# A two-layer hybrid model on one core: the first weight tile loaded ahead of x, x in two transfers with its norm weights, and the mixer's tiles multiplied high parts first

## The reference

```python
def rmsnorm(x, g):
    xf = x.astype(jnp.float32)
    y = xf * lax.rsqrt(jnp.mean(xf * xf, axis=-1, keepdims=True) + EPS)
    return (y * g.astype(jnp.float32)).astype(x.dtype)

def short_conv_mixer(h, w_in, conv_w, w_out):
    bg, cg, v = jnp.split(h @ w_in, 3, axis=-1)
    return (bg * causal_dwconv(cg * v, conv_w)) @ w_out

def conv_ffn(h, w_up, conv_w, w_down):
    u = causal_dwconv(h @ w_up, conv_w)
    a, g = jnp.split(u, 2, axis=-1)
    return (jax.nn.silu(a) * g) @ w_down

...
    for layer in range(DEPTH):
        if layer < N_A:
            x = x + short_conv_mixer(rmsnorm(x, mix_norm[layer]), a_w_in[i], a_conv[i], a_w_out[i])
        else:
            ...
            x = x + nsa_mixer(rmsnorm(x, mix_norm[layer]), b_w_qg[i], b_w_o[i], kv, rel_bias)
        x = x + conv_ffn(rmsnorm(x, ffn_norm[layer]), ffn_up[layer], ffn_conv[layer], ffn_down[layer])
    return rmsnorm(x, final_norm)
```

## Time and profile before

| what | value |
|---|---|
| median of three runs | 632.47 us (631.91 to 633.13) |
| the profiled execution's own time | 633.22 us |
| its span, first to last instruction | 631.5 us |
| PE busy | 610.9 us, 97% |
| DVE, ACT, POOL busy | 485.1, 388.6, 59.4 us |
| mean granted TensorE clock | 0.994 |
| DMA, mean over the span | 173 GB/s |

### The profile page before, as it was taken

The page is one execution under the profiler, slowest core; times in us unless marked ns, Lnnn a source line. Parts: engine busy times, 40 slices in busy tenths (PEclk is TensorE's granted clock), DMA queues, the critical chain, the costliest instruction groups (busy, mean ns, idle before and its releaser), DMA issues.

```text
span 631.5 us, 11277 instructions
## 1 busy us (share of the span) xinstructions
PE 610.9 (97%) x3738; PEld 534.1 (85%) x3738; DVE 485.1 (77%) x939; ACT 388.6 (62%) x708; POOL 59.4 (9%) x78
## 2 busy tenths in 40 slices
PE   7999999999999999999999898998999999999995
PEld 7999997888888888888989776777888888888884
DVE  4787756788888777777878789847788888777865
ACT  6644445666666666668556478717766666666644
POOL 0110002000000000011131144421000000000010
PEclk8999999999999999999999999999999999999998
DMA  8797432465656555761476400033365555555531
GB/s 310 290 336 241 179 133 100 166 203 194 205 201 202 199 189 179 287 241 34 146 245 214 142 2 2 1 101 133 118 206 193 209 201 207 192 178 195 199 101 66
DMA packets 30640, 109.55 MB, mean 173 GB/s; under 512 B 3419, under 2 KB 3691, under 8 KB 30476
## 3 DMA queue, kind: packets, MB, share of 16 engines
q1 hardware_dynamic: 30044, 106.97, 48.6%
q0 software_dynamic: 560, 2.12, 0.9%
HBM read 108.00 MB, written 1.07 MB: 173 GB/s over the span
## 4 chain that ended last, share of the span: by engine, by line
PE 88%; DVE 5%; ACT 3%; issue 2%; POOL 1%; DMA 1%; SPq 0%; DVEq 0%; ACTq 0%
PE bank L1129 24%; PE bank L1090 15%; PE bank L1091 15%; PE bank L1092 15%; PE bank L1133 13%; POOL work L486 1%; PE bank L1109 1%; DVE work L1013 1%; PE bank L1362 1%; DMA staged<-in_a_up 1%; ACT work L533 1%; PE bank L1320 1%; PE bank L1150 1%; PE bank L1110 1%; ACT w_hi L529 1%
## 5 line engine op out<-in xcount | busy, mean ns | idle before, releaser
L746 DVE TENSOR_TENSOR w_lo<-staged,w_hi 128x1024 fp32r<-128x1024 f32 x191 | 236.6, 1247 | 41.9 <-ACT w_hi L529 41.9
L529 ACT ACTIVATE w_hi<-staged 128x1024 fp32r<-128x1024 f32 x197 | 199.8, 1046 | 26.6 <-PE bank L1092 15.7
L1129 PE MATMUL bank<-gx,w_hi 128*128 128x512 f32 x672 | 167.2, 391 | 0.0
L1129 PEld LDWEIGHTS bank<-gx,w_hi 128*128 128x128 f32 x672 | 123.2, 188 | 23.8
L1133 PEld LDWEIGHTS bank<-gx,w_lo 128*128 128x128 f32 x672 | 91.7, 190 | 6.6
L1133 PE MATMUL bank<-gx,w_lo 128*128 128x256 f32 x672 | 93.7, 282 | 0.0
L1090 PE MATMUL bank<-w_hi,y 128*128 128x512 f32 x208 | 81.5, 392 | 0.0
L1091 PE MATMUL bank<-w_lo,y 128*128 128x512 f32 x208 | 81.5, 392 | 0.0
L1092 PE MATMUL bank<-w_hi,y 128*128 128x512 f32 x208 | 80.9, 389 | 0.0
L615 ACT ACTIVATE work<-work,params 128x256 f32<-128x256 f32 x96 | 44.2, 504 | 57.4 <-DVE work L847 39.2
L1090 PE MATMUL bank<-gx,w_hi 128*128 128x256 f32 x256 | 73.4, 287 | 2.6 <-DVE w_lo L746 2.1
(11 more groups left out here) (160 smaller groups left out, 818.7 us busy)
## 6 DMA issues: line engine op xcount, KB each, us to landing
staged<-in_f_up SPq DMA_DIRECT2D x88, 512.0 KB, 5.2
staged<-in_f_down SPq DMA_DIRECT2D x44, 512.0 KB, 3.3
staged<-in_a_up SPq DMA_DIRECT2D x24, 512.0 KB, 7.3
staged<-in_b_up SPq DMA_DIRECT2D x24, 512.0 KB, 4.3
staged<-in_a_down SPq DMA_DIRECT2D x8, 512.0 KB, 3.5
staged<-in_b_down SPq DMA_DIRECT2D x8, 512.0 KB, 4.2
bias<-bias_rows POOLq DMA_DIRECT2D x1, 2048.0 KB, 11.5
bias<-in_xT SPq DMA_DIRECT2D x4, 256.0 KB, 5.2
```

The costliest lines, as they stand in the source:

```text
L529: nc.scalar.activation(w_hi[:, q["slot"], 0:n], staged[:, s, 0:n], ACT.Copy).then_inc(hi, 1)
L746: nc.vector.tensor_tensor(w_lo[:, q["slot"], 0:n], staged[:, s, 0:n], w_hi[:, q["slot"], 0:n].bitcast(F32), ALU.subtract).then_inc(lo, 1)
L1129: nc.tensor.matmul(dst, w_hi[:, s, kt * P:kt * P + P], gx[:, kt, :], start=kt == 0, stop=False, skip_group_check=True)
```

## The change

It has four parts. The order in which SP issues the first loads is another: the first weight tile stands ahead of x, and the small parameters behind tile (1, 0). The transposed x comes in two transfers of four tiles each instead of four of two, and the first carries the eight columns of norm weights in front, which `norm_a` now reads instead of `params`; its lines are 4128 bytes long, those of the second 4096. `norm_a` handles tile (0, 0) ahead of the x tiles on ACT and DVE, and ACT puts tile (1, 0) between the two squares. `product` keeps its old order for piece (0, 0) alone; every other piece waits for `w_hi` only, issues its 16 matmuls with `w_hi`, then waits for `w_lo` and issues the other eight. PE makes piece (1, 0) ahead of `spread`, and `WARM` goes from 18 to 13.

```diff
-WARM = 18
+WARM = 13
...
-        x_first = bias[:, 0:KT, :]
+        x_lines = bias[:].rearrange("p h t -> p (h t)")[:, 0:KT + KT * T]
+        x_first = x_lines[:, KT:].rearrange("p (k t) -> p k t", k=KT)
...
             def x_tiles(b):
-                sp.dma_start(x_first[:, 2 * b:2 * b + 2, :], xT[:, 2 * b:2 * b + 2, :]).then_inc(x_landed[b], 16)
-
+                cols = slice(b * (KT + 4 * T), KT + (b + 1) * 4 * T)
+                sp.dma_start(x_lines[:, cols], xT[:, cols]).then_inc(x_landed[b], 16)
+
+            load("a", "up", 0, 0)
             x_tiles(0)
-            sp.dma_start(params[:], par).then_inc(par_landed, 16)
             x_tiles(1)
-            load("a", "up", 0, 0)
-            x_tiles(2)
-            x_tiles(3)
             load("a", "up", 0, 1)
             load("a", "up", 0, 2)
...
-            ups("a", 1)
+            load("a", "up", 1, 0)
+            sp.dma_start(params[:], par).then_inc(par_landed, 16)
+            load("a", "up", 1, 1)
+            load("a", "up", 1, 2)
...
             def norm_a():
 
-                act.wait_ge(par_landed, 16)
-                for b in range(4):
+                lead("a", "up", 0, 0)
+                for b in range(2):
                     act.wait_ge(x_landed[b], 16)
-                    for kt in (2 * b, 2 * b + 1):
+                    for kt in range(4 * b, 4 * b + 4):
                         nc.scalar.activation(gx_hi[:, kt, :], x_first[:, kt, :], ACT.Copy,
-                                             scale=gain(GAIN_OF["a"], kt)).then_inc(gx_hi_done, 1)
-                    if b == 1:
-                        lead("a", "up", 0, 0)
+                                             scale=x_lines[:, kt:kt + 1]).then_inc(gx_hi_done, 1)
...
                     if t:
+                        lead("a", "up", 1, 0)
                         act.wait_ge(squared, 1)
...
-                for c in range(3):
+                for c in (1, 2):
                     lead("a", "up", 1, c)
+                act.wait_ge(par_landed, 16)
...
             def norm_a():
 
-                dve.wait_ge(par_landed, 16)
+                rest("a", "up", 0, 0)
                 for kt in range(KT):
...
-                    if kt == 3:
-                        rest("a", "up", 0, 0)
                 rest("a", "up", 0, 1)
                 rest("a", "up", 0, 2)
+                rest("a", "up", 1, 0)
                 dve.wait_ge(deviated, 1)
...
             def product(q, dst, xh, xl, first, move=0, fresh=None, hi_sem=None):
 
                 s = q["slot"]
+                if fresh is not None:
+
+                    pe.wait_ge(lo_up, q["n"] + 1 + move)
+                    for kt in range(KT):
+                        pe.wait_ge(fresh, hi_sem + kt + 1)
+                        mm = three(dst, w_hi[:, s, kt * P:kt * P + P], w_lo[:, s, kt * P:kt * P + P],
+                                   xh[:, kt, :], xl[:, kt, :], first and kt == 0, kt == KT - 1)
+                    mm.then_inc(used_up, 1)
+                    return
+                pe.wait_ge(hi_up, q["n"] + 1 + move)
+                for kt in range(KT):
+                    for n, xs in enumerate((xh, xl)):
+                        nc.tensor.matmul(dst, w_hi[:, s, kt * P:kt * P + P], xs[:, kt, :], start=first and kt == 0 and n == 0, stop=False,
+                                         skip_group_check=True)
+
                 pe.wait_ge(lo_up, q["n"] + 1 + move)
                 for kt in range(KT):
...
+                    mm = nc.tensor.matmul(dst, w_lo[:, s, kt * P:kt * P + P], xh[:, kt, :], start=False, stop=kt == KT - 1,
+                                          skip_group_check=True)
                 mm.then_inc(used_up, 1)
...
                     up_a(0)
+                    up_a(1, cs=(0,))
                     spread()
...
-                    up_a(1)
+                    up_a(1, cs=(1, 2))
```

More of the change, by code:

```diff
@@ L221, in build @@
         landed = [sem(f"landed{s}") for s in range(UP_SLOTS + 1)]
-        x_landed = [sem(f"x_landed{b}") for b in range(4)]
+        x_landed = [sem(f"x_landed{b}") for b in range(2)]
         par_landed, hot_landed, bias_landed = sem("par_landed"), sem("hot_landed"), sem("bias_landed")
@@ L749, in norm_a @@
             def norm_a():
-                dve.wait_ge(par_landed, 16)
+                rest("a", "up", 0, 0)
                 for kt in range(KT):
                     dve.wait_ge(gx_hi_done, kt + 1)
-                    dve.wait_ge(x_landed[kt // 2], 16)
-                    nc.vector.scalar_tensor_tensor(gx_lo[:, kt, :], x_first[:, kt, :], gain(GAIN_OF["a"], kt),
+                    dve.wait_ge(x_landed[kt // 4], 16)
+                    nc.vector.scalar_tensor_tensor(gx_lo[:, kt, :], x_first[:, kt, :], x_lines[:, kt:kt + 1],
                                                    gx_hi[:, kt, :].bitcast(F32), ALU.mult, ALU.subtract).then_inc(gx_lo_done, 1)
-                    if kt == 3:
-                        rest("a", "up", 0, 0)
                 rest("a", "up", 0, 1)
                 rest("a", "up", 0, 2)
+                rest("a", "up", 1, 0)
                 dve.wait_ge(deviated, 1)
                 nc.vector.reciprocal(rstd_t[:, 0:2], rstd_t[:, 2:4]).then_inc(rstd_done, 1)
-                for c in range(3):
+                for c in (1, 2):
                     rest("a", "up", 1, c)
+                dve.wait_ge(par_landed, 16)
                 dve.wait_ge(rstd_spread, 1)
@@ L1110, in both, with up_a @@
                 return nc.tensor.matmul(out_ap[:, 0:T], w_lo[:, s, cols], gx_hi[:, kt, :], start=False, stop=stop, skip_group_check=True)
-            def up_a(k, i=0):
-                fresh = (gx_lo_done, 0) if k == 0 else (None, None)
+            def up_a(k, i=0, cs=range(3)):
                 if k >= 2:
                     pe.wait_ge(scaled["a"], k - 1 + PER["a"] * i)
-                for c in range(3):
+                for c in cs:
+                    fresh = (gx_lo_done, 0) if (k, c) == (0, 0) else (None, None)
                     dst = bank[2 * (k % 2) + c // 2][:, c % 2 * T:(c % 2 + 1) * T]
@@ L1519 @@
     arrays = {
-        "xT": np.asarray(x)[0].T.reshape(KT, P, T).transpose(1, 0, 2), "xt": np.asarray(x)[0].reshape(2, P, D).transpose(1, 0, 2),
+        "xT": np.concatenate([feat(mix_norm[0]), np.asarray(x)[0].T.reshape(KT, P, T).transpose(1, 0, 2).reshape(P, KT * T)], 1), "xt": np.asarray(x)[0].reshape(2, P, D).transpose(1, 0, 2),
         "par": par, "final": np.broadcast_to(np.asarray(final_norm), (P, D)), "hot": one_hot_of_distances(),
```

## The result

The changed kernel takes 629.49 us (median of five runs, 629.36 to 629.55) against 632.47 us before (631.91 to 633.42, five runs). The ratio of the runs is 0.9945, 95% interval 0.9934 to 0.9956: faster by 0.55%, some 3 us. The profiled execution takes 629.55 us with a span of 627.8 us; before it was 633.22 and 631.5, so these two lie 3.67 us apart. By the medians alone it is 2.98 us, or 0.47%. The forecast was 630.7 us, a gain of 1.77 us. The measured median lies within the forecast's range of 629.0 to 631.8, but the ratio, taken from 632.47, gives 629.0, which is the range's lower end. The gain is 1.7 times the forecast one by the medians and 2 times by the ratio.

What follows compares the result with a forecast made beforehand. PE, busy 97% of the span, was taken as the bound, with time to save at the start. Order 0, `params` 0 and first matmul −1.7 us from the 632.47 us median gave 630.8, forecast as 630.7, range 629.0 to 631.8.

Steps and rivals of the forecast that it cites:

- order of matmuls: In `product`, 16 matmuls with `w_hi` before eight with `w_lo`: priced at 0, cover worth up to 1 us only with the fast clock.
- `params`, later: At the start, `params` moved behind tile (1, 0), its first reader coming after the taps of unit 0: priced at 0.
- landing of the first weight tile: At the program's start, the first weight tile was to land at 5.5 us, between bounds of 5.1 and 5.8.
- term of 1.7 us: First matmul of `product`: PE was to start at 8.4 us instead of 10.12, 1.7 us earlier.
- case A: First piece on PE: the first 16 matmuls run at the slow clock again; 630.7 us, range 630.0 to 631.4, chance 0.50.
- What bounds the kernel, and where a gain can come from: Whole kernel: PE is busy 97% of the span, so the gain at 14.4 us, behind the first piece, reaches the end.
- B: First piece on PE: PE keeps 2.4 GHz and the piece ends 2.9 us earlier; 629.6 us, chance 0.30.
- The short warm-up, `spread`, the late root: Start of PE: shorter warm-up costs nothing; root comes one `lead` later (1.06 us), `spread` one piece later (2.9 us).
- C: Start: first weight tile lands at 4.1 us, PE starts at 7.0, gain 4.2 us; 628.3 us, chance 0.05.
- D: First piece: with fewer warm-up matmuls PE stays slow for 5.5 us, gain only 0.7 us; 631.8 us, chance 0.11.
- E: Piece (1, 0) waits for its weights, needed by 17.3 us; slower, 634.5 us if they land at 21 us; chance 0.04.

## Why the prediction was off

**What failed.** The sum was 0 (order of matmuls) + 0 (`params`, later) − 1.7 us. The step that failed is the landing of the first weight tile, 5.5 us with a lower bound of 5.1, measured 4.68. It made the term of 1.7 us too small: the first product came 2.54 us earlier. By the idle time that it gave, it also made case A, the slow clock, the likelier one. The clock stayed at 1.00, so the first piece took 1.09 us less, and the order of matmuls, put at 0, was worth 1.2 us. That the kernel without the new order takes 630.71 us, where I forecast 630.7, is luck: it is a case with a quick landing and the fast clock, and neither was in the forecast.

**What bounds the kernel, and where a gain can come from.** Right. Only the start of stage `a` changed on PE, no later wait moved, and the gain at the 25th matmul (3.63 us) is the gain at the end (3.67 us between the two profiled executions).

**When the first weight tile lands.** The prediction said that the tile "can't beat the first 256 KB of x", which set the lower bound, and took 5.5 us. The tile landed at 4.68, and at 4.1 to 4.6 in the seven other profiles with it in front. The bound took the time of one tensor's transfer for another's. It also took the 183 GB/s between 2 and 4 us for the rate of that time, while it was the rate with x in front; with the weight tile there it is 310. In these profiles the size decided little: 256 or 516 KB of x in front take 4.3 us alike, and 260 or 516 KB of x behind the weight tile land about 5.1 us behind their issue alike. What follows them in the queue differs, so this is no clean comparison of sizes. Whether x is slow for its place in HBM, for a first touch or for another reason is open; no run separates these. The Trainium skill's 2.0 us and 436 GB/s ("DMA: Bandwidth & Descriptors", "Anatomy of one DMA") gave 4.0 us, an estimate; the measured 4.1 to 4.7 is nearer to that than my 5.5 is, although its fit is for transfers issued by another path.

**The first matmul.** The steps behind the landing were right. With 4.68 put in place of 5.5, `w_lo` comes at 7.0 (measured 7.02), the first `gx_lo` at 7.5 (7.45), PE at 7.6 (7.58). So the term of 1.7 us was mis-sized by the landing alone. That x would be ready in time was an estimate (6.8 us, measured 6.38), and `params` behind x is part of what made it true: with `params` in front, x comes 1.3 to 1.6 us later. The sum had booked "0 (`params`, later)". Moving `params` has no cost of its own, but what it makes room for is worth as much at the start, and more through the clock.

**The clock.** I forecast case A, slow again, at 0.50, and B, clock kept, at 0.30. B happened: in all four profiles of the changed kernel with 13 or 18 warm-ups or x in four, and by their times in all 21 runs of these. The reason that I gave for B was an idle time under 2.14 us, and the profiles had 1.42, 0.39, 0 and 1.8. That fits, but it isn't shown to be the cause, since 2.90 and 3.57 us kept the clock in two other profiles. I had also taken the slow level as what 2.14 us lead to, from a single execution; 28 of 62 runs of the kernel before kept the clock. B's price, 2.9 us, with the landing at 4.68 in place of 5.5 is 3.7, and the profiles give 3.63 at the 25th matmul. That price holds against a run of before with its clock lost. I subtracted it, and the 1.7, from the median, which mixes both sets; against one with its clock kept the gain is 2.6 to 2.8 us.

**The order of matmuls.** I priced it at 0, with "up to 1 us only in the fast case". Measured in the fast case: 1.2 us with the new loads, 0.4 us on the kernel before. The cover that I named is real, and PE would have waited without it at piece (0, 1) only. The price at 0 hung on case A.

**The short warm-up, `spread`, the late root.** Priced at nothing, and worth nothing: 18 warm-ups give the same time, and `spread` moved ahead as planned (19.60 us on PE, two microseconds behind the reciprocal at 17.52).

**The rivals.** C, the quick landing, was the right mechanism and too large: the tile landed at 4.68 us instead of 4.1, x held the first product at 7.58 instead of 7.0, and the time was 629.5 us instead of 628.3. D, a longer slow stretch, is what happens with five warm-ups. E did not occur: `w_hi` of tile (1, 0) was done at 16.13 us, 0.6 us ahead of when PE wanted it (16.73).

**The sum by parts, from the runs.** The loads and `norm_a` give 1.6 us (630.66 against 632.26, the mean of the kernel before with its clock kept, on the same chip). The order of matmuls on top of them gives 1.2. Together that is 2.8 us, of the 2.6 to 2.8 measured. Where the kernel before loses its clock, 0.9 to 1.3 us come on top, and the changed kernel lost it in none of its 10 runs.

## What to carry to other kernels

At the start of a program, price a load from rows of that place and of that tensor; another tensor's time was no bound here, and 249 KB in front of the transfer needed next cost 1.3 to 1.6 us. Where a median mixes two sets of times, look at the granted clock of each run before taking one profile as the kernel before: it may hide a stall that the other set has. When a chain is shortened at one end, ask at once which piece is late next; here the order by high parts was worth nothing on one profile and 1.2 us once the loads were early.

## What the runs showed of the hardware

As the first transfer of the program x took 4.3 to 4.4 us to land, with 256 KB (three profiles) and with 516 KB (one), and a 512 KB weight tile 3.3 to 3.8 us (eight profiles). In the second place the two took the same, 5.2 us for the weight tile and 4.9 to 5.2 us for x. Between 2 and 4 us the DMA moved 142 to 208 GB/s with x in front and 310 or more with the weight tile there.

The granted-clock column does not show the slow stretch from the program's start: with five warm-ups it reads 1.00, while the matmuls stand 0.21 us apart until about 13.5 us. The clock can fall behind the idle time, with PE already at work again: with 24 warm-ups PE started at 10.25 us and the pace fell at about 11.2 us. An idle time of 2.0 to 2.3 us in front of the product ended in the lower clock in three profiled executions, and 2.90 and 3.57 us did not in two others. So the length of the idle time alone does not decide it.
